# Second block of a two-block model: the order of attention, its gates, the values' projection and the branch's chains

## The reference, cut to what matters

```python
xn = rmsnorm(h, norm1_gain[i]); proj = xn @ w_in[i]
q, k, v, u, gates = jnp.split(proj, splits, axis=-1)
q = rope(rmsnorm(q, q_norm_gain[i]), cos, sin)        # 8 heads, 2 components of 64
k = rope(rmsnorm(k, k_norm_gain[i]), cos, sin)
o = diff_attention(q, k, v, lam)                      # a = softmax(0) - lam * softmax(1), causal
o = rmsnorm(o, subln_gain[i]) * (1.0 - lam_init)      # v has 128 columns a head
attn_branch = o.reshape(bsz, seq, V_COLS) @ w_attn_proj[i]
s = s5_layer(u, ...)            # scan, then g = gelu(y); g * sigmoid(g @ w_glu + b_glu)
ssm_branch = s @ w_ssm_proj[i]
g_attn, g_ssm = jnp.split(jax.nn.sigmoid(gates), 2, axis=-1)
h = h + (g_attn * attn_branch + g_ssm * ssm_branch) @ w_out[i]
```

## Time and profile before

| | us |
|---|---|
| median of three runs (2375.74 to 2376.28) | 2375.84 |
| the profiled execution's own time | 2377.99 |
| its span, first to last instruction | 2376.2 |
| mean granted TensorE clock, share of full | 0.969 |
| TensorE busy | 2248.2 |
| VectorE / ScalarE / POOL busy | 1078.8 / 895.4 / 886.2 |

### The profile page before, as it was taken

How to read it: one execution, slowest core, us unless ns; L and a number is a source line. 1 busy time by engine, 2 the same in 40 slices (tenths; PEclk the granted TensorE clock), 3 DMA queues, 4 the chain that set the end, 5 groups by cost and what they waited for, 6 DMA issues and landing times.

```text
span 2376.2 us, 28595 instructions
## 1 busy us (share of the span) xinstructions
PE 2248.2 (95%) x10212; PEld 1731.2 (73%) x10212; DVE 1078.8 (45%) x1761; ACT 895.4 (38%) x1247; POOL 886.2 (37%) x274
## 2 busy tenths in 40 slices
PE   8999999999999999999999988868988789999999
PEld 6765688888878665888888865544765578788887
DVE  7753242222248443422122486764166562455445
ACT  5334362232243353632232413253355444333332
POOL 5422254434455222544344553220321135343433
PEclk9999999999999999999999989888999899999999
DMA  5412122232224111222323131111211122223232
GB/s 172 150 43 69 36 80 99 88 106 88 90 77 161 63 54 36 89 89 92 102 88 105 64 136 36 36 59 53 89 37 53 36 71 89 89 89 105 88 101 76
DMA packets 110584, 195.02 MB, mean 82 GB/s; under 512 B 4752, under 2 KB 41872, under 8 KB 110224
## 3 DMA queue, kind: packets, MB, share of 16 engines
q1 hardware_dynamic: 109040, 191.21, 24.5%
q10 hardware_dynamic: 1440, 2.44, 0.3%
...
## 4 chain that ended last, share of the span: by engine, by line
PE 72%; issue 19%; DVE 3%; POOL 3%; ACT 1%; DMA 1%; SPq 0%; ACTq 0%; POOLq 0%; DVEq 0%
PE bank L662 57%; PE bank L763 4%; PE bank L772 4%; POOL w_lo L509 3%; PE bank L836 1%; PE bank L799 1%; PE bank L968 1%; PE bank L827 1%; PE bank L716 1%; PE bank L725 1%; DVE b_pow L2128 0%; PE bank L999 0%; PE bank L998 0%; DMA lam<-in_lam 0%; PE bank L862 0%
## 5 line engine op out<-in xcount | busy, mean ns | idle before, releaser
L509 POOL TENSOR_TENSOR w_lo<-raw,w_hi 128x2048 fp32r<-128x2048 f32 (+1 forms) x167 | 740.3, 4433 | 1382.9 <-ACT w_hi L1253 1382.8
L662 PE MATMUL bank<-act_hi,w_hi 128*128 128x512 f32 x1488 | 605.6, 407 | 12.0 <-DVE act_lo L1895 4.4
L662 PE MATMUL bank<-act_lo,w_hi 128*128 128x512 f32 x1488 | 587.7, 395 | 0.0
L662 PE MATMUL bank<-act_hi,w_lo 128*128 128x512 f32 x1488 | 586.8, 394 | 0.0
L1253 ACT ACTIVATE w_hi<-raw 128x2048 fp32r<-128x2048 f32 (+1 forms) x170 | 314.1, 1848 | 632.3 <-PE bank L662 603.1
L662 PEld LDWEIGHTS bank<-act_hi,w_hi 128*128 128x128 f32 x1488 | 284.5, 191 | 93.4 <-issue 27.0
L662 PEld LDWEIGHTS bank<-act_lo,w_hi 128*128 128x128 f32 x1488 | 284.7, 191 | 61.9 <-issue 5.3
L662 PEld LDWEIGHTS bank<-act_hi,w_lo 128*128 128x128 f32 x1488 | 284.2, 191 | 61.7
L662 PE MATMUL bank<-h_hi,w_hi 128*128 128x512 f32 x736 | 296.4, 403 | 18.0 <-DVE h_lo L1895 17.7
L662 PE MATMUL bank<-h_lo,w_hi 128*128 128x512 f32 x736 | 293.0, 398 | 0.0
L662 PE MATMUL bank<-h_hi,w_lo 128*128 128x512 f32 x736 | 292.8, 398 | 0.0
...
## 6 DMA issues: line engine op xcount, KB each, us to landing
...
raw<-in_w_up SPq DMA_DIRECT2D x44, 512.0 KB, 4.5
...
raw<-in_w_down SPq DMA_DIRECT2D x22, 512.0 KB, 4.2
...
```

What stands on the lines that cost most here:

```text
L509: pool.tensor_tensor(m.w_lo[slot][:, 0:n], m.raw[slot][:, 0:n], m.w_hi[slot][:, 0:n].bitcast(F32), ALU.subtract).then_inc(s["split_ready"], 1)
L662: mm = pe.matmul(o, ll if i == 2 else lh, rl if i == 1 else rh, start=first and n == 0, stop=last and n == len(steps) - 1)
```

## The change

The values' projection is cut into its two groups. One stands between scan and GLU, the other between GLU and the branch's projection, with banks of their own (`V2_BANKS`, `GLU_BANKS`). Steps are numbered 32 to 59 from there on (values 32 and 44, GLU 40, branch projection 52). The jobs' table `Q_JOBS` gives every second step from 12 to 30 one job, then steps 32, 35 to 43 and 46 to 57. The values lie where x was parked from (`x_at`), so ScalarE's queue loads x back behind attention.

In attention, transposes are of step i-3 and go to banks 6 and 3 in turn; the product with the values is of step i-4; there are four buffers for each component. The mean of o squared has bank 2, VectorE reads it a step later. A gate unit has the whole depth (eight chunks) of 256 columns. Its pieces go at the steps of `GATE_STEPS`, a block of gates takes two pieces, and blocks use banks 0 and 1 in turn. The last four gates' sigmoid and the products `ssm` times gate 4 to 7 stand behind the loop.

```diff
-    m.v2 = ar("v2", [P, NT, D], 72)
+    m.v2 = put("v2", [P, NT, D], at=x_at)
     m.s_hi, m.s_lo = (ar(f"sum{i}", [P, 4, T], 72 + 8 * i, F32R) for i in range(2))
-    m.att = [ar(f"att{i}", [P, T], 32 + 2 * i) for i in range(4)] + [ar(f"att{4 + i}", [P, T], 88 + 2 * i) for i in range(3)]
-    m.att += [put(f"att{7 + i}", [P, T], at=late_at + 2048 * i) for i in range(3)]
+    m.att = [ar(f"att{i}", [P, T], 32 + 2 * i) for i in range(4)] + [ar(f"att{4 + i}", [P, T], 88 + 2 * i) for i in range(3)] + [m.cos]
+    m.pt2 = [put("pt2_0", [P, T], at=late_at), m.sin]
+    m.o_root, m.o_square = (put(name, [P, T], at=late_at + 2048 * (1 + i)) for i, name in enumerate(("o_root", "o_square")))
...
         column_group(w, 0, g * GROUP)
+    column_group(w, 0, 2 * D)
     column_group(a["w_glu_2"], 0, 0, rows_in=SW)
+    column_group(w, 0, 2 * D + GROUP)
     for g in range(2):
         column_group(a["w_ssm_proj_2"], 0, g * GROUP, rows_in=SW)
 
-    sp.wait_ge(s["gelu"], 4)
-    sp.dma_start(m.x[:].rearrange("p k t -> p (k t)"), m.x_park).then_inc(s["x_back"], 16)
     sp.wait_ge(s["glu_done"], 1)
     sp.dma_start(m.mask[:], a["mask"]).then_inc(s["table_loaded"], 16)
-    for g in range(2):
-        column_group(w, 0, 2 * D + g * GROUP)
-    for g in range(4):
-        column_group(w, 0, 3 * D + SW + g * GROUP)
+    for g in range(2 * D // G2):
+        load((into(KD, G2), rows(w, 0, 0, KD, 3 * D + SW + g * G2, G2)))
     for w in (a["w_attn_proj_2"], a["w_out_2"]):
         for g in range(2):
             column_group(w, 0, g * GROUP)
...
+    between.extend([lambda p=p: hook(p) for p in range(V2_AT[0], PROJ_AT + 8)])
+    token_major(GROUP)
     pe.wait_ge(s["h_lo"], c.up("h_lo", 4))
-    feature_major(4, 1, ah=m.h_hi[0], al=m.h_lo[0])
+    feature_major(4, 1, ah=m.h_hi[0], al=m.h_lo[0], to=GLU_BANKS)
+    token_major(GROUP, V2_BANKS[1])
     pe.wait_ge(s["h_lo"], c.up("h_lo", 4))
-    between.extend([lambda p=p: hook(p) for p in range(32, 40)])
     for g in range(2):
         feature_major(4, 1, ah=m.h_hi[1], al=m.h_lo[1])
-    for g in range(2):
-        token_major(GROUP)
...
-    def gate_piece(i):
-
-        g, u, b = i // 8, i // 4 % 2, i % 4
-        if b == 0:
-            gate_weights[:] = weights(next_unit(), KU, GROUP)
+    def gate_piece(n):
+
+        blk, half = gate_part(n)
+        if n % 4 == 0:
+            gate_weights[:] = weights(next_unit(), KD, G2)
         wh, wl = gate_weights
-        cols = slice(b * P, (b + 1) * P)
-        accumulate(b, bank[b][:], [(wh[:, k, cols], wl[:, k, cols], m.act_hi[:, u * KU + k, :], m.act_lo[:, u * KU + k, :])
-                                   for k in range(KU)], u == 0, u == 1, b == 3)
+        cols = slice(blk % 2 * P, (blk % 2 + 1) * P)
...
-            mm.then_inc(s["full6"], 1)
         if 3 <= i < n_steps + 3:
             h, t = divmod(i - 3, NT)
+            to = TURN_BANKS[i % 2]
+            pe.wait_ge(s["probs_scaled"], c.up("probs_scaled"))
+            fill(to)
+            for kc in range(t + 1):
+                mm = pe.transpose(bank[to][:, kc * P:(kc + 1) * P], m.att[(i - 3) % 4][:, kc * P:(kc + 1) * P], m.ident)
+            mm.then_inc(s[f"full{to}"], 1)
+        if i >= 5 and (i - 5) % NT == NT - 1:
+
+            pe.wait_ge(s["o_squared"], c.up("o_squared"))
+            one(O_MEAN, m.avg128, m.o_square[:])
+        if 4 <= i < n_steps + 4:
+            h, t = divmod(i - 4, NT)
             if t == 0:
                 fill(7)
 
             pe.wait_ge(s["probs_turned"], c.up("probs_turned"))
             for kc in range(t + 1):
                 mm = pe.matmul(bank[7][:, t * P:(t + 1) * P], m.v2[:, kc, h * P:(h + 1) * P],
-                               m.att[6 + (i - 3) % 2][:, kc * P:(kc + 1) * P], start=(kc == 0), stop=(kc == t))
+                               m.pt2[(i - 4) % 2][:, kc * P:(kc + 1) * P], start=(kc == 0), stop=(kc == t))
             if t == NT - 1:
                 mm.then_inc(s["full7"], 1)
-        if i < n_steps:
-            gate_piece(i)
-        if i >= 4 and (i - 4) % NT == NT - 1:
-
-            pe.wait_ge(s["o_squared"], c.up("o_squared"))
-            one(6, m.avg128, m.att[9][:])
+        if i in GATE_STEPS:
+            gate_piece(GATE_STEPS.index(i))
 
     feature_major(4, ready=parts_ready)
     feature_major(4)
...
 
+TURN_BANKS, O_MEAN = (6, 3), 2
+ATT_STEPS = N_HEADS * NT + 6
+
+GATE_STEPS = [*range(27), 28, 29, 30, 32, 33]
+
+
+def gate_part(n):
+
+    unit, part = divmod(n, 4)
+    within, half = divmod(part, 2) if n < 28 else (part % 2, part // 2)
+    return 2 * unit + within, half
+
+
+def gates_done(i):
+
+    return [gate_part(n)[0] for n, step in enumerate(GATE_STEPS) if step + 1 == i and gate_part(n)[1]]
+
+
 def heads_split(i):
 
-
-    last = N_HEADS * NT + 4
-    return [N_HEADS - 1] if i == last else list(range(max(0, 2 * (i - last + 4) - 1), 2 * (i - last + 4) + 1)) if last - 4 <= i < last else []
+    return {32: [0], 33: [1], 34: [2, 3], 35: [4, 5], 36: [6], 37: [7]}.get(i, [])
 
...
 
+Q_JOBS = [*range(12, 32, 2), 32, *range(35, 44), *range(46, 58)]
+
+
 def q_jobs_at(p):
 
-    if p < 32:
-        return [p - 12] if p >= 12 else []
-    return list(range(20 + 3 * (p - 32) // 2, 20 + 3 * (p - 31) // 2))
-
-
+    return [Q_JOBS.index(p)] if p in Q_JOBS else []
+
+
+V2_AT, GLU_AT, PROJ_AT = (32, 44), 40, 52
+V2_BANKS, GLU_BANKS = ((0, 1, 2, 3), (1, 2, 3, 0)), (4, 5, 6, 0)
...
 
+    def v2_out(g, t):
+
+        evac(V2_BANKS[g][t], m.v2[:, t, g * GROUP:(g + 1) * GROUP], scale=m.rstd[:, t:t + 1])
+
+    hi()
     for q in range(4):
         act.wait_ge(s["skip_added"], q + 1)
         link(act.activation(m.uT[:, q, :], m.uT[:, q, :], ACT.Gelu_apprx_tanh), "gelu")
...
-    for p in range(8):
-        if p == 4:
-
+    for p in range(V2_AT[0], PROJ_AT + 9):
+        for g in range(2):
+            if 5 <= p - V2_AT[g] < 9:
+                v2_out(g, p - V2_AT[g] - 5)
+            if p == V2_AT[g] + 4:
+                hi("half")
+            if p == V2_AT[g] + 8:
+                hi()
+        if p == GLU_AT + 4:
+            for b, of in enumerate(GLU_BANKS):
+                evac(of, m.hid[:, b, :], ACT.Sigmoid, bias=m.scol[:, SC["b_glu"] + b:SC["b_glu"] + b + 1])
+            act.preload_act_table_set(LN_EXP)
             hi()
-        evac(p % 4, m.ssm[:, p, :])
-        for n in q_jobs_at(32 + p):
+            for b in range(4):
+                act.wait_ge(s["glu_ready"], c.up("glu_ready"))
+                copy_hi(in_chunks(m.h_hi[1][:, b, :]), in_time(m.uT[:, b, :]), "h_hi")
+        if p > PROJ_AT:
+            at = p - PROJ_AT - 1
+            evac(at % 4, m.ssm[:, at, :])
+            if at == 3:
...
+
+    def gate_sigmoid(g):
+
+        freed(0)
+        freed(1)
+        for b in range(4):
+            gate = m.gates[:, 4 * g + b, :] if g < 2 else m.gate[:, b, :]
+            act.activation(gate, gate, ACT.Sigmoid).then_inc(s["gate_ready"], 1)
 
     n_steps = N_HEADS * NT
-    for i in range(n_steps + 5):
-        if i >= 8 and i % 8 == 0 and i <= n_steps:
-            use(0, 1, 2, 3)
-        if i >= 9 and i % 8 == 1:
-
-            g = i // 8 - 1
-            for b in range(4):
-                freed(b)
-                gate = m.gates[:, 4 * g + b, :] if g < 2 else m.gate[:, b, :]
-                act.activation(gate, gate, ACT.Sigmoid).then_inc(s["gate_ready"], 1)
+    for i in range(ATT_STEPS):
+        for blk in gates_done(i):
+            use(blk % 2)
+        if i in (9, 17, 25):
+            gate_sigmoid(i // 8 - 1)
             act.preload_act_table_set(LN_EXP)
         if i < n_steps:
             if i % 4 == 1:
-                hi("half" if i // 4 % 2 else None)
+                hi(1 if i > 4 else None)
             n = (i % NT + 1) * P
             for comp in range(2):
                 use(4 + comp)
                 freed(4 + comp)
                 at = 2 * (i % 2) + comp
-                pr = m.att[3 * comp + i % 3][:, 0:n]
+                pr = m.att[4 * comp + i % 4][:, 0:n]
                 act.activation(pr, pr, ACT.Exp, scale=-1.0, bias=m.nmax[:, at:at + 1], accum_out=m.rowsum[:, at:at + 1]
                                ).then_inc(s["probs"], 1)
-        if 2 <= i < n_steps + 2:
-            n = ((i - 2) % NT + 1) * P
-            full(6)
-            link(act.activation(m.att[6 + (i - 2) % 2][:, 0:n], bank[6][:, 0:n], ACT.Copy), "probs_turned")
-            act.sem_inc(s["free6"], 1)
-        if 3 <= i < n_steps + 3 and (i - 3) % NT == NT - 1:
-
-            h = (i - 3) // NT
+        if 3 <= i < n_steps + 3:
+            n = ((i - 3) % NT + 1) * P
+            of = TURN_BANKS[i % 2]
+            full(of)
+            link(act.activation(m.pt2[(i - 3) % 2][:, 0:n], bank[of][:, 0:n], ACT.Copy), "probs_turned")
+            act.sem_inc(s[f"free{of}"], 1)
+        if 4 <= i < n_steps + 4 and (i - 4) % NT == NT - 1:
+
+            h = (i - 4) // NT
             full(7)
             if h:
                 act.wait_ge(s["o_normed"], h)
```

(82 more changed lines are left out.)

49 lines of the change are left out of this document (10 added, 39 removed).

## The result

The change took 2313.46 us in the median of four runs (2312.01 to 2317.5) against 2376.06 for the kernel before on the same chip: ratio 0.9739, interval 0.9722 to 0.9756, 62.6 us faster. The forecast was 2306 with a range of 2284 to 2340. The profiled execution has a span of 2312.7 us, 63.5 less than before.

What follows compares the result with a forecast made beforehand. TensorE was taken as nearly always busy but slowed by waits and the lower clock that follows them. Terms -36 - 10 - 36 + 6 = -76, less 6 given back, made -70: 2306 us, range 2284 to 2340.

Steps and rivals of the forecast that it cites:

- S: Projections of q and k beside the scan, 145.6 us: ten jobs leave, bank 7's wait goes; about 110 us, -36.
- G: GLU, branch's projection and values, 135.1 us: h_lo waits go, a wait for bank 7 comes; 125 us, -10.
- T: Attention with its end, 204.8 us: waits at heads' ends and for scaled probabilities go; 169 us, -36.
- the 18.3 us: Attention, heads' ends: seven waits of transposes for bank 6, holding the mean of o squared; claimed to go, 18.3 us.
- the 14.1: Attention: six waits for scaled probabilities, 14.1 us, claimed to go because a lag of three gives one more step.
- Behind attention: Attention projection's start: tables and four sigmoids ahead of w_hi make it 5.2 us later; +6, bounds 0 and +9.
- (a): Rival: ScalarE's queue binds in attention, 0.8 us in each of 32 steps, 25 us come back: 2331 us; chance 0.2.
- (b): Rival: nearly every wait goes and the clock recovers in all stages, -119, 2257 us; chance 0.1.
- (c): Rival: a table switch on ScalarE costs more than its load, four gate blocks 2.6 us longer each, 2316 us; chance 0.03.
- (d): Rival, slower: each of 22 jobs in the values, GLU and branch stage meets POOL's block, 101 us, 2407 us; chance 0.03.
- (e): Rival: values do not cover the GLU's chains, h_lo late by ScalarE's order, 17.7 us and slow clock stay, 2330; chance 0.02.
- the allowance of 6: Whole kernel: 6 us given back from the sum of -76, since the placement puts every operation as early as possible.

Runs made afterwards that it cites:

- best3: The changed kernel plus four moves against its waits, runs of 32-row matmuls halved, and banks 1, 2, 0, 3 for the second values: 2277.34 us, ratio 0.9586.

## Why the prediction was right, and where not
**S: sign right, 13 us too much.** The own work of 103.6 us was right: best3 runs the stage in 104.7 us at a clock of 1.00 with one wait of 1.3 us. The step that failed is "which leaves 103.6 [...] About 110": it let all slow clock go with the waits. I read the stage's 0.92 as time that follows waits, but the clock stayed at 0.89 with 8.6 us of waits instead of 14.5, and cutting the runs of 32-row matmuls gave 9 us with every wait left in. Beside its waits the stage holds 10.6 us over its own work, where the sum left 0.7. Slow clock behind a run that had no wait ahead could have been read in the trace before. The rest is the last states, 7.3 us instead of 3, less 1.4 at the squares. I placed VectorE's operations in order, but did not ask whether POOL's block would lie on them; two blocks did (one operation of 4.38 us, one of 4.99).

**G: right.** The values cover both chains, and without them 15 to 17 us come back. The wait at step 47 was forecast at 6.6 and is 6.4, by the queue that the forecast laid out. The 3 us put at further collisions with POOL were not seen as such: in their place stand a wait of 2.7 at step 52, which I had not laid out and which a bank's number removed, and one of 1.2. Waits are 10.3 in all for 9.6 forecast, and what lies beside them is 6.7 for the 4 given to the clock; that is the miss of 3. The upper bound's "such a 1.2 us delay" has no row.

**T: size right, reasons partly wrong.** 169 forecast, 167.7 measured. But "the mean of o squared has bank 2 of its own [...] so the 18.3 us go" and "the lag of three [...] the 14.1 go" both failed as causes: each alone can be taken back at no cost. The mean's move ahead of the step's piece hides its root and brings it ahead of the sigmoids on ScalarE; at the old place an own bank still loses 17 us, 13 of them through the sigmoids' place. The whole order of attention is worth 26 of T's 37 us. That both can go at once with the mean at its new place was not tried. The forecast had the edit in its order rows and did not price the place. For scaled probabilities, 3.2 of the 14.1 us are back with the old lag and banks; the gates' units are the likely cause of the rest, not a shown one. A small slip of the sum: "some 0.4 a head" makes 3.2, and the sum has 2.

**Behind attention: right**, +4.9 for +6, with a wait of 6.9 for 5.8, by the queue named; moving one w_hi ahead of the sigmoids left a wait of 2.0.

**The rivals.** (a) ScalarE's queue did bind, at three steps and not at 32. (b) did not come with the change (2313, not 2257); with the further moves best3 is at 2277. (c) A table switch costs its load and no more: the sigmoids begin at 1848.23, 0.02 after the load ends, and in the first head the load at 1709.84 starts 0.02 after the operation ahead of it ends, so 1.28 us and no drain on either side. The drain of about 1380 ns that the Trainium skill gives ("ScalarE: Activation LUTs", section "What ACT_TABLE_LOAD costs") does not show here either. (d) POOL's block did meet VectorE's queue, twice where it mattered, not at each job. (e) fell: no wait for h_lo. 

**The sum.** That it came within 6.5 us (7.5 by the medians) is in part luck. S missed by 13.2 and G by 3.2; the allowance of 6 for places not laid out took up less than half of that, and 3.7 more lie ahead of S, 2.6 of them in a part that the change does not touch.
